# Second output projection by row panels, with the four group norms taken one by one

## What is computed

```python
mixed = jnp.concatenate([rms_norm(y_a, out_norm[l, 0]), rms_norm(y_b, out_norm[l, 1]),
                         rms_norm(y_c, out_norm[l, 2]), rms_norm(y_d, out_norm[l, 3])], axis=-1)
x = x + mixed @ w_out[l]
gu = rms_norm(x, norm_ffn[l]) @ w_gate_up[l]
x = x + (jax.nn.silu(gu[..., :D_FF_2]) * gu[..., D_FF_2:]) @ w_down[l]
```

## Time and profile before

| | us |
|---|---|
| median of 3 runs | 864.1 |
| lowest, highest | 864.06, 871.87 |
| profiled execution | 869.24 |
| its span | 867.4 |
| TensorE busy in it | 817.1 (94%) |
| mean granted TensorE clock | 0.927 |

### The profile page before, as it was taken

One profiled execution on the slowest core, in us unless ns is written; L12 is line 12 of the kernel. 1 busy time (PEld: TensorE's weight loads), 2 busy tenths in 40 slices (PEclk: granted clock), 3 DMA queues, 4 the chain that ended last, 5 costly groups with the idle time before them and its releaser, 6 DMA issues.

```text
span 867.4 us, 14523 instructions
## 1 busy us (share of the span) xinstructions
PE 817.1 (94%) x5302; PEld 733.8 (85%) x5302; DVE 548.1 (63%) x1016; ACT 450.4 (52%) x849; POOL 62.9 (7%) x94
## 2 busy tenths in 40 slices
PE   3979997999899999999999999979889999999998
PEld 2679996889699889999999998958788899999997
DVE  3775434978759686666666675447766766666663
ACT  3455445565563565545454556066644654545552
POOL 7001002000034500000000020000000000000000
PEclk9579998999989799999999899569879999999999
DMA  8789864878639646666657475403205466565731
GB/s 266 248 223 299 262 184 137 246 220 249 209 115 297 188 140 198 195 179 185 191 172 196 97 188 159 128 28 95 74 26 169 131 185 190 173 196 173 203 105 49
DMA packets 194349, 151.07 MB, mean 174 GB/s; under 512 B 13298, under 2 KB 178600, under 8 KB 194176
## 3 DMA queue, kind: packets, MB, share of 16 engines
q1 hardware_dynamic: 188896, 143.61, 56.9%
q10 hardware_dynamic: 3760, 5.87, 1.8%
q0 software_dynamic: 1648, 1.00, 0.6%
HBM read 146.78 MB, written 3.41 MB: 173 GB/s over the span
## 4 chain that ended last, share of the span: by engine, by line
PE 79%; DVE 11%; ACT 5%; DMA 2%; issue 2%; ACTq 0%; DVEq 0%
PE ps L1833 19%; PE ps L1530 13%; PE ps L1531 12%; PE ps L1532 12%; PE ps L1835 10%; DVE w_lo L1018 3%; PE ps L1910 2%; ACT w_hi L657 1%; DMA arena<-in_x 1%; PE ps L1646 1%; PE ps L1768 1%; DVE sq L1101 1%; PE ps L1578 1%; PE ps L1746 1%; DVE sq L1075 1%
## 5 line engine op out<-in xcount | busy, mean ns | idle before, releaser
L1018 DVE TENSOR_TENSOR w_lo<-raw,w_hi 128x1024 fp32r<-128x1024 f32 (+3 forms) x223 | 270.7, 1233 | 104.8 <-ACT w_hi L657 104.5
L1833 PE MATMUL ps<-h,w_hi 128*128 128x512 f32 x704 | 254.0, 400 | 1.3 <-DVE h L1097 1.0
L657 ACT ACTIVATE w_hi<-raw 128x1024 fp32r<-128x1024 f32 (+3 forms) x223 | 227.0, 1038 | 30.8 <-PE ps L1532 9.1
L1835 PE MATMUL ps<-h,w_lo 128*128 128x256 f32 x704 | 199.3, 283 | 0.0
L1833 PEld LDWEIGHTS ps<-h,w_hi 128*128 128x128 f32 x704 | 133.1, 189 | 34.3 <-issue 1.7
L1530 PE MATMUL ps<-h,w_hi 128*128 128x256 f32 (+1 forms) x472 | 140.9, 299 | 6.4 <-DVE h L1097 2.2
L1531 PE MATMUL ps<-h,w_hi 128*128 128x256 f32 (+1 forms) x472 | 136.0, 288 | 0.0
L1532 PE MATMUL ps<-h,w_lo 128*128 128x256 f32 (+1 forms) x472 | 135.9, 288 | 0.0
L1835 PEld LDWEIGHTS ps<-h,w_lo 128*128 128x128 f32 x704 | 133.2, 189 | 0.1
L1530 PEld LDWEIGHTS ps<-h,w_hi 128*128 128x128 f32 (+1 forms) x472 | 92.9, 197 | 12.9 <-issue 10.1
L1530 PE MATMUL ps<-g_hi,w_hi 128*128 128x256 f32 x352 | 98.6, 280 | 0.0
(11 more groups left out here) (325 smaller groups left out, 1177.2 us busy)
## 6 DMA issues: line engine op xcount, KB each, us to landing
raw<-in_w_in SPq DMA_DIRECT2D x53, 512.0 KB, 5.1
raw<-in_w_ada SPq DMA_DIRECT2D x48, 512.0 KB, 4.6
raw<-in_w_down SPq DMA_DIRECT2D x44, 512.0 KB, 4.2
raw<-in_w_gate_up SPq DMA_DIRECT2D x44, 512.0 KB, 4.0
raw<-in_w_gate SPq DMA_DIRECT2D x22, 512.0 KB, 3.9
raw<-in_w_up SPq DMA_DIRECT2D x22, 512.0 KB, 5.0
raw<-in_w_o SPq DMA_DIRECT2D x8, 512.0 KB, 4.8
raw<-in_w_out SPq DMA_DIRECT2D x8, 512.0 KB, 3.6
```

Source lines behind the costliest of these rows:

```text
L657: A(w_hi[:, m % HL, 0:w], raw[:, n % RAW, 0:w], ACT.Copy).then_inc(hi_done, 1)
L1018: V.tensor_tensor(w_lo[:, m % HL, 0:w], raw[:, n % RAW, 0:w], w_hi[:, m % HL, 0:w].bitcast(f32), sub).then_inc(lo_done, 1)
L1833: T.matmul(bank[:, :], hi, h2[:, k, :, :].rearrange("p a b -> p (a b)"), start=(k == 0), stop=False, skip_group_check=True)
L1835: ins = T.matmul(bank[:, 0:SEQ], lo, h_hi[:, k, :], start=False, stop=(k == KC - 1), skip_group_check=True)
```

## The change

`w_out` is cut into row panels (`panel("wout", ...)` over `Y_ROWS` = 4, 5, 2, 3, 0, 1, 6, 7), so that a panel needs one chunk of `mix` only, and 8 output chunks accumulate in four banks (`ACC2`). The norms go group by group through small helpers. Group 0 (y_c, chunks 4 and 5) is done inside the attention loop: squares at x = 2, the sum over channels at x = 3, root at x = 4, reciprocal and spread at x = 5, scaling, `mix_hi` and `mix_lo` at x = 6. The last fill chunk moves from x = 7 to x = 6, and the first row panel takes its place in x = 7. Panels 1, 3 and 5 have the spread of group 1, 2 or 3 in their middle, and a `y_sums` behind panels 1 and 3 (that of group 1 stands before panel 1). GELU moves to x = 5 and the recurrence's root to x = 6. An activation on one column (`warm`) with `Exp` follows the root of x = 4 and the GELU. `x_ready` adds come after the last panel's banks (`wout_done`), the squares are summed by TensorE as in the first block, and `keep_awake` shrinks from 6 and 3 to 1 and 1.

The diff, without most unchanged lines:

```diff
@@ -73,7 +73,7 @@
 EARLY = 2
-FILL_AT = {0: 3, 1: 4, 2: 5, 3: 6, 4: 7, 5: 8, 7: 9}
+FILL_AT = {0: 3, 1: 4, 2: 5, 3: 6, 4: 7, 5: 8, 6: 9}
 ADA_FIRST, ADA_LAST = 2 * KC, 5 * KC
@@ -81,6 +81,7 @@
 ADA_STEP = (1, 2, 4, 5, 7, 8, 10, 11)
+Y_ROWS = (4, 5, 2, 3, 0, 1, 6, 7)
 MAGIC = 1.5 * 2.0 ** 23
@@ -203,8 +204,8 @@
         chunk("fill", w_in2, c)
-    for c in range(KC):
-        chunk("wout", I["w_out_2"], c * P)
+    for k in Y_ROWS:
+        panel("wout", [(0, 1, D, 0, D, cols(I["w_out_2"], 0, D, k, 1))])
     ffn_panels(1)
@@ -480,7 +481,6 @@
         L["fill"] += [output("fill", c) for c in range(EARLY, len(FILL))]
-        L["wout"] = [output("wout", c, ("x_ready", 24 + c + 1)) for c in range(KC)]
         L["ffn1"] = [output("ffn1", 0 if j == 0 else 3 * j - 1, ("g_sum", FC + j + 1)) for j in range(FC)]
@@ -507,7 +507,9 @@
                    sx[:, 0, 2:], sx[:, 1, 2:], s_b[:, 0, :], s_b[:, 1, :]]
-        Y_ORDER = (0, 1, 4, 5, 2, 3, 6, 7)
+        Y_SQ = (4, 6, 0, 2)
+        ACC2 = [ps[0], ps[1], ps[4], ps[5]]
+        Y_FAC = [ps[6][:, SEQ:512], ps[2][:, 0:SEQ], ps[3][:, 0:SEQ], ps[6][:, SEQ:512]]
         PAIRS = [(N1 + 2 * x, N1 + 2 * x + 1) for x in range(N2 // 2)]
@@ -952,6 +954,23 @@
+            def y_square(n):
+                for x in range(2):
+                    line(A(sq[:, Y_SQ[n] + x, :], yT[:, Y_ROWS[2 * n] + x, :], ACT.Square), "y_sq")
+            def y_root(n):
+                act.wait_ge(s("y_ss"), n + 1)
+                line(A(yrms[:, 2 * n:2 * n + 2], YSUM[:, 2 * n:2 * n + 2], ACT.Sqrt, scale=1.0 / GROUP, bias=eps_c), "y_rms")
+            def y_high(n):
+                for x in range(2):
+                    c = Y_ROWS[2 * n] + x
+                    act.wait_ge(s("y_ready"), 2 * n + x + 1)
+                    line(A(mix_hi[:, c, :], yT[:, c, :], ACT.Copy), "y_hi")
             for g in PAIRS[0]:
@@ -969,33 +988,45 @@
                     exps(b + 2)
-                else:
+                if x == 2:
+                    act.wait_ge(s("o_hi"), 20)
+                    y_square(0)
+                if x == 6:
+                    y_high(0)
+                if q is not None:
+                    fill(q)
+                if x == 4:
+                    y_root(0)
+                    line(A(warm, eps_c, ACT.Exp))
+                if x == 5:
                     line(A(lg, lg, ACT.Gelu_apprx_tanh), "lg_ready")
+                    line.settle()
+                    line(A(warm, eps_c, ACT.Exp))
+                if x == 6:
                     act.wait_ge(s("lru_w"), 1)
                     line(A(yT[:, 0:2, :], yT[:, 0:2, :], ACT.Sqrt), "lru_sqrt")
-                if q is not None:
-                    fill(q)
+            act.wait_ge(s("yb_ready"), 1)
+            y_square(1)
             o_copy(PAIRS[-1][0])
             o_copy(PAIRS[-1][1])
-            for n, c in enumerate(Y_ORDER):
-                if n == 0:
-                    act.wait_ge(s("ya_ready"), 1)
-                if n == 2:
-                    act.wait_ge(s("o_hi"), 24)
-                if n == 4:
-                    act.wait_ge(s("yb_ready"), 1)
-                line(A(sq[:, c, :], yT[:, c, :], ACT.Square), "y_sq")
-            act.wait_ge(s("y_ss"), 4)
-            line(A(yrms, YSUM, ACT.Sqrt, scale=1.0 / GROUP, bias=eps_c), "y_rms")
-            for n, c in enumerate(Y_ORDER):
-                act.wait_ge(s("y_ready"), n + 1)
-                line(A(mix_hi[:, c, :], yT[:, c, :], ACT.Copy), "y_hi")
+            y_root(1)
+            act.wait_ge(s("ya_ready"), 1)
+            y_square(2)
+            split.ahead(nth("wout", 0))
+            y_high(1)
+            act.wait_ge(s("o_hi"), 24)
+            y_square(3)
+            y_root(2)
+            split.ahead(nth("wout", 1))
+            y_high(2)
+            y_root(3)
+            split.ahead(nth("wout", 2))
+            y_high(3)
+            for n in range(3, KC):
+                split.ahead(nth("wout", n))
             for c in range(KC):
-                split.ahead(nth("wout", c))
-                if c == 0:
-                    act.wait_ge(s("y_lo"), 8)
                 square(c, 24)
@@ -1375,6 +1406,26 @@
+            def y_total(n):
+                dve.wait_ge(s("y_sq"), 2 * n + 2)
+                line(V.tensor_tensor(sq[:, Y_SQ[n], :], sq[:, Y_SQ[n], :], sq[:, Y_SQ[n] + 1, :], add), "y_tot")
+            def y_inverse(n):
+                dve.wait_ge(s("y_rms"), n + 1)
+                line(V.reciprocal(yrms[:, 2 * n:2 * n + 2], yrms[:, 2 * n:2 * n + 2]), "y_inv")
+            def y_scaled(n):
+                dve.wait_ge(s("y_fac"), n + 1)
+                for c in (Y_ROWS[2 * n], Y_ROWS[2 * n + 1]):
+                    line(stt(out=yT[:, c, :], in0=yT[:, c, :], scalar=vcol("out_norm_2", c), in1=Y_FAC[n], op0=mult,
+                             op1=mult), "y_ready")
+            def y_low(n):
+                for x in range(2):
+                    c = Y_ROWS[2 * n] + x
+                    dve.wait_ge(s("y_hi"), 2 * n + x + 1)
+                    line(V.tensor_tensor(mix_lo[:, c, :], yT[:, c, :], mix_hi[:, c, :].bitcast(f32), sub), "y_lo")
             dve.wait_ge(s("gate2_ready"), 1)
@@ -1386,6 +1437,12 @@
                     scores(b + 2)
+                if x == 3:
+                    y_total(0)
+                if x == 5:
+                    y_inverse(0)
+                if x == 6:
+                    y_scaled(0)
                 if x in FILL_AT:
@@ -1413,44 +1470,44 @@
                     probabilities(b + 2)
-            split.ahead(nth("wout", 0) - 1)
-            dve.wait_ge(s("lru_sqrt"), 1)
-            line(V.tensor_tensor(ia, ia, yT[:, 0:2, :], mult))
-            line.settle()
-            for c in range(2):
-                line(V.tensor_tensor_scan(xc[:, c, :], ra[:, c, :], ia[:, c, :], 0.0, mult, add))
-            line.settle()
-            dve.wait_ge(s("lg_ready"), 1)
-            line(V.tensor_tensor(yT[:, 0:2, :], xc, lg, mult), "ya_ready")
+                if x == 6:
+                    y_low(0)
             for c in range(2):
                      None if c == 0 else "yb_ready")
-            for n in range(4):
-                c = Y_ORDER[2 * n]
-                dve.wait_ge(s("y_sq"), 2 * n + 2)
-                line(V.tensor_tensor(sq[:, c, :], sq[:, c, :], sq[:, c + 1, :], add), "y_tot")
-            dve.wait_ge(s("y_rms"), 1)
-            line(V.reciprocal(yrms, yrms), "y_inv")
-            for n in range(KC + 2):
-                if n < KC:
-                    c = Y_ORDER[n]
-                    dve.wait_ge(s("y_fac"), n // 2 + 1)
-                    line(stt(out=yT[:, c, :], in0=yT[:, c, :], scalar=vcol("out_norm_2", c), in1=ps[n // 2][:, 0:SEQ],
-                             op0=mult, op1=mult), "y_ready")
-                if n >= 2:
-                    c = Y_ORDER[n - 2]
-                    dve.wait_ge(s("y_hi"), n - 1)
-                    line(V.tensor_tensor(mix_lo[:, c, :], yT[:, c, :], mix_hi[:, c, :].bitcast(f32), sub), "y_lo")
-            for c, l in enumerate(L["wout"]):
-                split.ahead(outputs[l])
-                await_out(dve, l)
-                line(V.tensor_tensor(xT[:, c, :], lin(l), xT[:, c, :], add), "x_ready")
-                if c >= 1:
-                    total(c - 1, 3)
-            total(KC - 1, 3)
+            dve.wait_ge(s("lru_sqrt"), 1)
+            line(V.tensor_tensor(ia, ia, yT[:, 0:2, :], mult))
+            y_total(1)
+            line.settle()
+            for c in range(2):
+                line(V.tensor_tensor_scan(xc[:, c, :], ra[:, c, :], ia[:, c, :], 0.0, mult, add))
+            line.settle()
+            dve.wait_ge(s("lg_ready"), 1)
+            line(V.tensor_tensor(yT[:, 0:2, :], xc, lg, mult), "ya_ready")
+            y_inverse(1)
+            y_total(2)
+            y_scaled(1)
+            y_low(1)
+            split.ahead(nth("wout", 0))
+            y_total(3)
+            y_inverse(2)
+            y_scaled(2)
+            y_low(2)
+            split.ahead(nth("wout", 1))
+            y_inverse(3)
+            y_scaled(3)
+            y_low(3)
+            for n in range(2, KC):
+                split.ahead(nth("wout", n))
+            for c in range(KC):
+                if c == KC - 2:
+                    dve.wait_ge(panel_used, nth("wout", KC - 1) + 1)
+                elif c % 2 == 0:
+                    dve.wait_ge(s("wout_done"), c // 2 + 1)
+                line(V.tensor_tensor(xT[:, c, :], ACC2[c // 2][:, SEQ * (c % 2):SEQ * (c % 2) + SEQ], xT[:, c, :], add),
+                     "x_ready")
             inverse(3)
@@ -1597,7 +1654,7 @@
-                if k == 1:
+                if k in (1, 3):
@@ -1935,6 +1992,36 @@
             line(T.matmul(ps[7][:, 48:48 + NCMP], half1[:, :], kcq[:, 0:NCMP], start=True, stop=True), "kc_ss")
+            def y_sums(n):
+                pe.wait_ge(s("y_tot"), n + 1)
+                if n >= 1:
+                    pe.wait_ge(s("y_rms"), n)
+                    pe.wait_ge(s("y_ready"), 2)
```

(46 more changed lines are left out.)

8 lines of the change are left out of this document (4 added, 4 removed).

## The result

The kernel after the change takes 862.37 us (median of 13 runs, 857.59 to 867.33); the kernel before, 868.45 (13 runs, 864.06 to 871.87). The forecast was 859.0 against 864.1 before, a ratio of 0.9941, and its range 854.5 to 863.8 is 0.989 to 0.9997 as a ratio. A second comparison is told with the experiments.

What follows compares the result with a forecast made beforehand. TensorE, busy 94% of the span, was taken as the bound, with gains only where it waits or runs slowly. Terms: -5.65 + 0.5 = -5.1 us, from 864.1 to 859.0 us on the medians' scale; range 854.5 to 863.8.

Steps and rivals of the forecast that it cites:

- The loop's end moves by 3.85 us: End of second block's attention loop: work added to VectorE makes panel 0 start 3.85 us later than the old chunk.
- VectorE's wait for `w_hi`: In x = 5, VectorE's split waits 1.1 us for ScalarE, held up by the root and its table loads.
- The table loads: ScalarE, x = 4 and 5: each switch counted at 1.28 us; GELU's loads hidden with half a microsecond of cover.
- rival 3: In the loop: each added table switch costs double, 4.7 us more in all, 863.7 us; chance 0.08.
- Panel 0 itself: First row panel in x = 7: taken as 5.1 us at clock 0.50, bounds 2.83 and 5.1.
- rival 1: Loop's end: panel 0 fast (2.3 us) and the 1.1 us wait for ScalarE may vanish, 855.6 us; chance 0.20.
- Behind the loop: Seven panels 19.8, sums and spreads 2.7, stall 1.85: 24.35 us, projection issued 5.65 us sooner.
- rival 2: Projection: mid-panel spreads come late, each group exposing about 1 us, 862.0 us; chance 0.12.
- The gap before panel 6: Projection: panel 6 waits 1.85 us, as VectorE's split of it stands behind `y_low(3)`.
- rival 4: Projection: the clock does not come back, 2.27 us per slow panel; five give 870.4 us; chance 0.05.
- Rival 5: Loop's end: row panels cannot start in the loop, panel 0 blocks the gathers, shift about 9 us, 864.1 us; chance 0.05.
- The tail: Norm behind the projection, up to the first up panel: 0.5 us more than before, bounds 0 and 1.3.

Runs made afterwards that it cites:

- gelu6: The changed kernel with GELU back from x = 5 to x = 6, before the recurrence's root, without its extra table load; 861.03 us (one run).
- early_hi: The changed kernel with ScalarE's split of x = 5 moved ahead of the root and its table loads in x = 4; 862.06 us (one run).
- before_again: The kernel before the change, unedited, profiled a second time; 867.76 us (one run).
- rows_only: The kernel before with row panels and the changed kernel's tail, all four norms together behind the loop; 865.17 us, ratio 0.9978 to the kernel before.
- no_loop: The changed kernel with group 0's norm and panel 0 behind the loop, last fill chunk in x = 7; 866.07 us, ratio 0.9986 to the kernel before.
- split6: The changed kernel with VectorE's split of panel 6 moved ahead of group 3's scaling; 865.1 us (one run).
- behind: The changed kernel with panel 6's split ahead of group 3's scaling and VectorE's last two ffn splits behind the adds; 863.1 us (one run).
- awake3: The changed kernel with six `keep_awake` matmuls behind the factor instead of two; 856.81 us (one run).
- after_again: The changed kernel, unedited, measured and profiled a second time; 860.87 us (8 runs), ratio 0.992 to the kernel before.
- best3: The changed kernel with splits of x = 5, x = 6, panel 6 and the last two ffn splits moved, and six `keep_awake`; 853.63 us, ratio 0.9865 to before.

## Why the prediction was right, and where two of its terms were not

The mechanism was right and the sum too (-5.1 forecast, about -6 measured; by the stretch -5.9 between the first two profiles, -3.9 between the second two), but two of its terms were off with opposite signs.

- **The loop's end moves by 3.85 us:** right. Panel 0 starts 39.4 after the fill chunk of x = 1, the old chunk started at 35.4: 4.0. On the forecast's scale it starts at 628.5, for 628.4. VectorE's wait for `w_hi` was 1.42 for 1.1 (on the forecast's scale, 2.65 later than in the rows, VectorE is ready at 614.1 and the split starts at 615.5; forecast were 614.2 and 615.3); the other terms have their sizes.
- **The table loads:** each is 1.28 long, the activation starts 0.01 to 0.02 behind it, and the next load 0.02 behind that, so rival 3 is out. The drain that the Trainium skill adds ("ScalarE: Activation LUTs", What ACT_TABLE_LOAD costs) is not seen at any of the switches in x = 4 to 6; the measurement decides. GELU in x = 5 costs nothing (gelu6); its cover is as thin as said (early_hi).
- **"Panel 0 itself: ... I take 5.1 for it":** this step failed. It took 3.0 in the first profile (628.86 - 625.86, both first matmuls, as the 5.12 of the old chunk is measured), at a granted clock of 1.00, as rival 1 has it. I had carried over the clock before the old chunk, though the fill chunk that moved to x = 6 keeps TensorE dense closer to the end. That this is the reason is not shown by an edit of its own, but the profiles fit: in the four without a chunk in x = 6 (before, before_again, rows_only, no_loop) the last chunk met a fallen clock each time (its matmuls start over 4.9, 3.8, 3.8 and 3.7 us, against 2.8 at full clock), in the nine with one panel 0 met it three times, for 1.0 to 1.6 us of loss, never 2.3. The lower bound of 2.83 was the better value. Rival 1 as a whole (8.5 us) didn't come, since its other half, the vanished wait for ScalarE, failed and the tail took 1.8.
- **Behind the loop:** from the end of the gathers to the last product 24.25 for 24.35. Panels 2 and 4 wait for nothing, so rival 2 is out. The gap before panel 6 is 1.60 for 1.85, ended by VectorE's `w_lo`, and split6 shows that it is the queue's order. The clock stays at 1.00 from 585 to 658: rival 4 is out. Rival 5 is out by panel 0's place, and no_loop shows what it would be worth. The prediction put some 1.1 us of the old projection down to the clock at its start. before_again loses 1.4 to 1.5 there at full clock, to the pace at which the column form gets its chunks (rows_only), so that term had the wrong cause, near its right size.
- **The tail, "0.5 more than before; bounds 0 and 1.3":** this step failed, it is 1.8. The reason given for it ("the adds to `xT` start late ... inside the sums' own time") named the right place and priced it at nothing. The sums wait for the squares and these for the adds, so adds that start only as the last product does delay the sums by 0.7 (they start 0.82 behind it, against 0.12 in behind). Then the clock falls within the sums: 0.8 more on their length, and 0.7 more from their end to the first gate panel (663.51 - 659.81 = 3.7, for 665.89 - 662.85 = 3.0). behind is the test: with two splits moved the tail is 12.3. The 0.7 of waiting is shown by it; the two terms of the clock went the same way, in one profile each. The `keep_awake` matmuls that went cost something too, where the prediction had them at nothing: the first gate panel takes 4.9 to 5.6 without them, 4.5 to 4.7 with six behind the factor (awake3).

The clock that stayed gave 2.1 more than forecast and the tail took 1.3 more; that they nearly cancel is luck. With the tail of behind and all else as in after, the stretch would be 7.9 us shorter than before, and the forecast 2.8 too small; with the fallen clock of after_again, the forecast is 0.7 to 1.2 too large.

Of the cause of the gain: the two theories of the expectations were the hidden chain and the recovered clock. The chain is shown, by no_loop, which brings one group's part of it back, and rows_only, which has all of it: each loses most of the gain. Some 1.4 us of what stays in rows_only is a third cause, the row form itself, which only the rival of that run had. The clock adds or takes 1.5 from one execution to the next. Of the cures, the order at panel 6 was worth 1.5 us, the place of the adds 2 or more, and the two edits in the loop 2.2 together (early_hi alone 0.5); best3 collects them.

## What to carry to other kernels

When a panel's wait is cured, look at what its engine does next in its queue: work that is wanted late (here two weight splits) must stand behind work that someone already waits for (the adds), or the cure comes back as a wait one stage later. Hiding a serial norm in a loop can take away the whole hole behind the loop (9.7 us here, for 4.0 by which the loop ends later) if one group can be done early enough for the first panel, and the others can follow in mid-panel; spreading the norm behind the loop alone brought next to nothing here. When the operand is still being made, cut the weights so that a panel asks for one piece of it: the column form asked faster than VectorE could deliver. Price a shift in a full queue by who reads its results, not by the engine's own idle time.

## What the runs showed of the hardware

The clock can fall within the 32 matmuls of the norm's sums, which have one output column each, while TensorE shows no idle time. They take 3.63 us where the clock holds, 4.45 in after, and 5.97 in split6 behind a wait of 1.48. In after's windows the engine is busy throughout 656 to 660 and the clock falls from 1.00 to 0.54.

A wait straight before them is not the whole reason. In the second block, where the sums come directly behind the last product, the clock holds in three of three profiles (3.6 each in rows_only, behind and best3); behind a wait of 0.5 to 1.5 they took 3.73 to 5.97 in eight. But in the first block the same sums stand directly behind dense work in all thirteen profiles, and took 3.7 to 3.9 in nine, 4.6 in before, 5.3 in no_loop, 6.1 in split6 and 6.4 in after_again:

```profile
294.72 6.35 PE L1662 MATMUL ps<-ones,sq 128*128 128x1 f32 x32
```

In the last three TensorE had stood idle for 0.3 to 0.8 us between 6 and 3 us before the sums (in after_again it is busy for 2.16 of 3.00), in the other ten not at all in the 12 us before them. So idle time some us back goes with a longer time of these matmuls here, but not always: before had none, and after, gelu6 and no_loop, all with the gap of 1.6 before panel 6, took 4.45, 5.57 and 3.73. What decides it was not found.

A table load is 1.28 us to the hundredth for Sqrt, Exp and GELU; it starts 0.02 behind a short activation, and its own activation 0.01 to 0.02 behind it.
